# Block and sparse attention of a two-block transformer in steps of two heads: TensorE's order of scores, weight tile, transposes and sums

## What is computed

```
moba (8 heads), one block of 256 keys, so the selected part is empty:
  p = softmax(where(kpos <= qpos, q k^T * scale, -inf));  y_a = p v
nsa (8 heads), per head:
  o_cmp = softmax(q kc^T) vc                  15 compressed keys
  o_slc = softmax(q_rot k_slc^T) v_slc        all blocks are selected
  o_win = softmax(q_rot k_win^T) v_win        window of 512
  out   = g0 * o_cmp + g1 * o_slc + g2 * o_win
```

## Time and profile before

| | |
|---|---|
| median of 3 runs | 2458.36 us (2456.95 to 2459.53) |
| the profiled execution's own time | 2455.22 us |
| its span | 2453.6 us |
| TensorE busy | 2315.1 us (94%) |
| VectorE (DVE) busy | 1648.4 us (67%) |
| ScalarE (ACT) busy | 1225.6 us (50%) |
| TensorE's mean granted clock | 0.978 of full speed |
| DMA | 461.97 MB, mean 188 GB/s |

### The profile page before, as it was taken

The page is one execution under the profiler, slowest core; times in us unless marked ns, Lnnn a source line. Parts: engine busy times, 40 slices in busy tenths (PEclk is TensorE's granted clock), DMA queues, the critical chain, the costliest instruction groups (busy, mean ns, idle before and its releaser), DMA issues.

```text
span 2453.6 us, 40748 instructions
## 1 busy us (share of the span) xinstructions
PE 2315.1 (94%) x14828; PEld 2054.1 (84%) x14828; DVE 1648.4 (67%) x2387; ACT 1225.6 (50%) x1701; POOL 76.3 (3%) x143
## 2 busy tenths in 40 slices
PE   3999998899999999989899999999999999999999
PEld 2888987888887888879888889789888898898888
DVE  7888666567778787666576566656765666557665
ACT  3445466454445445565354455545544555465443
POOL 0100000000000000000000000000000000000000
PEclk9999998899999999999899999999999999999999
DMA  8876554445665874645445544333555353334553
GB/s 329 287 281 219 199 201 153 170 155 206 257 239 211 289 276 168 224 148 186 147 156 187 188 170 174 121 120 139 187 189 188 139 206 121 108 130 167 206 182 109
DMA packets 74827, 461.97 MB, mean 188 GB/s; under 512 B 8448, under 2 KB 8592, under 8 KB 28464
## 3 DMA queue, kind: packets, MB, share of 16 engines
q1 hardware_dynamic: 53712, 383.28, 43.2%
q0 software_dynamic: 19376, 72.00, 8.2%
q10 hardware_dynamic: 1584, 4.62, 0.5%
HBM read 458.82 MB, written 1.05 MB: 187 GB/s over the span
## 4 chain that ended last, share of the span: by engine, by line
PE 82%; DVE 5%; ACT 5%; issue 4%; DVEq 2%; DMA 1%; ACTq 1%
PE ps L713 20%; PE ps L439 15%; PE ps L441 15%; PE ps L440 15%; PE ps L715 10%; DVE wlo L1563 1%; DMA adat<-in_ada 1%; ACT whi L1056 1%; PE ps L547 1%; PE ps L529 1%; PE ps L561 1%; PE ps L594 1%; DVE bufA L1696 1%; DVEq L1665 1%; ACT set_a L1104 0%
## 5 line engine op out<-in xcount | busy, mean ns | idle before, releaser
L1563 DVE TENSOR_TENSOR wlo<-raw,whi 128x2048 fp32r<-128x2048 f32 x360 | 823.7, 2291 | 243.7 <-ACT whi L1056 226.7
L1056 ACT ACTIVATE whi<-raw 128x2048 fp32r<-128x2048 f32 x359 | 686.1, 1912 | 224.0 <-PE ps L441 220.1
L713 PE MATMUL ps<-hx,whi 128*128 128x512 f32 x2112 | 750.8, 399 | 10.5 <-DVE hx L1666 6.7
L715 PE MATMUL ps<-hx,wlo 128*128 128x256 f32 x2112 | 593.8, 281 | 0.0
L713 PEld LDWEIGHTS ps<-hx,whi 128*128 128x128 f32 x2112 | 398.3, 189 | 109.8 <-DVE hx L1666 7.2
L439 PE MATMUL ps<-hx,whi 128*128 128x256 f32 (+1 forms) x1424 | 423.0, 297 | 6.1 <-DMA blk<-in_block 2.9
L440 PE MATMUL ps<-hx,whi 128*128 128x256 f32 (+1 forms) x1424 | 408.6, 287 | 0.0
L441 PE MATMUL ps<-hx,wlo 128*128 128x256 f32 (+1 forms) x1424 | 408.1, 287 | 0.0
L715 PEld LDWEIGHTS ps<-hx,wlo 128*128 128x128 f32 x2112 | 400.3, 190 | 2.1
L439 PEld LDWEIGHTS ps<-hx,whi 128*128 128x128 f32 (+1 forms) x1424 | 278.9, 196 | 15.9 <-issue 8.0
L440 PEld LDWEIGHTS ps<-hx,whi 128*128 128x128 f32 (+1 forms) x1424 | 278.7, 196 | 4.7 <-issue 4.3
(11 more groups left out here) (274 smaller groups left out, 3043.5 us busy)
## 6 DMA issues: line engine op xcount, KB each, us to landing
raw<-in_w SPq DMA_DIRECT2D x360, 1024.0 KB, 4.8
adat<-in_ada POOLq DMA_DIRECT2D x128, 512.0 KB, 4.7
raw<-in_ada SPq DMA_DIRECT2D x4, 512.0 KB, 8.2
blk<-in_block POOLq DMA_DIRECT2D x2, 990.5 KB, 5.0
x<-in_x POOLq DMA_DIRECT2D x1, 1024.0 KB, 9.9
raw<-in_ada ACTq DMA_DIRECT2D x2, 512.0 KB, 14.8
set_b<-in_ada SPq DMA_DIRECT2D x2, 512.0 KB, 12.5
set_b<-in_ada ACTq DMA_DIRECT2D x2, 512.0 KB, 18.6
```

The costliest lines, as they stand in the source:

```text
L713: mm(ps[:, bank + i, :].rearrange("p (a s) -> p a s", a=2), whi[:, slot, col:col + P], hx[:, :, k, :], start=(k == 0), stop=False)
L715: last = mm(ps[:, bank + i, 0:S], wlo[:, slot, col:col + P], hhi[:, k, :], start=False, stop=(k == KD - 1))
L1056: A(whi[:, slot, :], raw[:, slot, :], ACT.Copy).then_inc(*T.counts("hi_ready"))
L1563: tt(wlo[:, slot, :], raw[:, slot, :], whi[:, slot, :].bitcast(F32), ALU.subtract)\
```

## The change

TensorE gets a second function, `attend_twos`, for block and sparse attention. An odd step has only what stands beside it. An even step s has the scores of s and s+1, what stands beside it, the turns of s-2 and s-1, and then the sums of s-4 and s-3. In sparse attention the tiles and rotations of TensorE's `beside_nsa` move from the odd steps to the even steps ahead of them. The programs of ACT, DVE, SyncE and GpSimd are the same; latent and differential attention still go through `attend`.

```diff
--- before.py
+++ after.py
@@ -597,6 +597,24 @@
                     mm(o[i][:, 128:256], ins.values(units[i], 1), bufC[:, i, 256:384], start=False, stop=True,
                        skip_group_check=True).then_inc(*T.counts("o_ready"))
 
+            def attend_twos(ins, beside, before=lambda u: None, first_turn=lambda: None):
+
+
+                for s in range(ins.units + 3):
+                    if s % 2:
+                        beside(s)
+                        continue
+                    if s < ins.units:
+                        scores(ins, (s, s + 1))
+                    if s == 2:
+                        first_turn()
+                    beside(s)
+                    if 2 <= s <= ins.units:
+                        turn(ins, s - 2)
+                        turn(ins, s - 1)
+                    if s >= 4:
+                        weigh(ins, s - 4, "pt_ready", before)
+
             def attend(ins, beside, before=lambda u: None, first_turn=lambda: None):
                 for s in range(ins.units + (2 if ins.fused else 3)):
                     if s < ins.units:
@@ -790,7 +808,7 @@
                         slot = tile()
                         features(open_fill(), slot, width=128, chunks=1).then_inc(*T.counts("tile_used"))
 
-                attend(moba, beside_moba)
+                attend_twos(moba, beside_moba)
                 pe.wait_ge(*T.nth("pj_out", T.n["fills"]))
 
                 def rotate_q(i):
@@ -974,14 +992,14 @@
                 pe.wait_ge(*T.nth("rope_done", T.n["rot_ready"]))
 
                 def beside_nsa(s):
-                    if s in (3, 5, 7, 9):
-                        i = (s - 3) // 2
+                    if s in (2, 4, 6, 8):
+                        i = (s - 2) // 2
                         rotate(c2("perm_half"), set_b[:, 2 * i:2 * i + 2, :], ps[:, 6, :])
-                    if s in (1, 3):
+                    if s in (0, 2):
                         project("tokens")
-                    elif s in (5, 7):
+                    elif s in (4, 6):
                         project("features")
-                    elif s in (9, 11, 13, 15):
+                    elif s in (8, 10, 12, 14):
                         merge_gate()
 
                 def compressed(u):
@@ -993,7 +1011,7 @@
                                         skip_group_check=True)
 
 
-                attend(nsa, beside_nsa, compressed, lambda: pe.wait_ge(*T.next("ct_out")))
+                attend_twos(nsa, beside_nsa, compressed, lambda: pe.wait_ge(*T.next("ct_out")))
                 pe.wait_ge(*T.nth("pj_out", T.n["fills"]))
                 wait_pairs()
                 pe.wait_ge(*T.nth("rope_done", T.n["rot_ready"]))
```

## The result

The kernel in steps of two heads takes 2511.32 us (median of 4 runs, 2511.07 to 2511.66) against 2458.82 us (4 runs, 2456.95 to 2459.53): ratio 1.0218, 95% interval 1.0203 to 1.0234, **52.5 us slower**. The forecast was 2504 us (2484 to 2520), that is +45.7 us. The profiled spans are 2509.7 and 2453.6 us, 56.1 us apart.

The account below looks back on a forecast made before the run. TensorE was taken as the bound, losing time where it stands still. Sparse waits 26.0, block waits 10.7 and clock 9 us gave +45.7 us on the profiled execution, 2500.9; with 3.1 us to the median, 2504 us, range 2484 to 2520.

Parts of the forecast that it names:

- Idle time inside sparse attention: Inside sparse attention: new TensorE waits ahead of rotations and scores in steps 4, 6, 8 and 12, 11.0 us per layer.
- the sum of 4.7 us: Sparse attention: time from the start of turn s-2 through turn, exponentials, norms and rope until the rope is done.
- The waits for norms that it saves: Sparse attention: the second turn would find its norms done behind a whole tile, saving 3.6 us per layer.
- The end of sparse attention: Last two turns, last sums and last pair would wait 3.0, 2.9, 1.0 and 0.95 us, together 7.85 against 2.28.
- Block attention: Middle costs nothing; last two turns and last sums wait 3.3, 3.7 and 1.3 us, 5.4 us more idle per layer.
- The clock: TensorE's clock halves behind new waits near or above 2 us: six falls taken, 9 us, bounded by 0 and 24.
- two in each sparse stretch: Clock falls assumed for each sparse attention stretch, beside one in each block stretch, six in all.
- the waits of step 6: Sparse attention: wait ahead of the rotation, put at 1.6 us and not among the waits that could lower the clock.
- all 16 waits: New waits near or above 2 us in block and sparse attention, eight per pair of stretches; all paying costs 24 us.
- Masks and ends pay, ropes don't: Rival: sparse rotations don't wait for ropes, only masks and the ends cost; 2485 us, chance 0.12.
- Every wait pays the clock: Rival: TensorE runs slow for 3 us after each of 16 new waits; 2519 us, chance 0.09.
- the forecast's own case: Waits in sparse attention and at block attention's ends plus six clock falls; 2504 us, bounds 2489 to 2519, chance 0.71.

Follow-up runs that it names:

- whole order: Against the kernel before: sparse attention alone in two-head steps, ordered even head's turn, rotation, sums, tile, odd head's turn; 2452.43 us, ratio 0.9975.
- the best one: The whole order plus matmuls on unused data in waits at the ends of block, latent and sparse attention and behind sparse; 2436.31 us, 0.9919 to the kernel before.
- rope first: The changed kernel with DVE's rope moved ahead of the odd head's norms in sparse attention; 2497.18 us, ratio 1.0160 to the kernel before.
- even turn first: The sparse-only kernel with the even head's turn alone moved ahead of rotation and tile; 2483.95 us, ratio 1.0110 to the kernel before.
- sparse-only kernel: The kernel before with the new two-head order in sparse attention alone, block attention in the old order; 2499.37 us, ratio 1.0164.

## Why the prediction was right

Size and sign were right, and the mechanism was the one forecast.

- *Idle time inside sparse attention.* Forecast 3.1, 1.6, 2.05, 2.2, 2.05; measured 3.02, 2.00, 2.09, 2.07, 2.09. Only the rotation of step 6 is off: it starts 5.06 us behind its turn, not 4.7. DVE's product with the gate starts 0.61 us behind the reciprocal there (1577.23 and 1577.84), in step 4 only 0.25 us, which is the difference. The handover from one engine to the next, which the prediction read as 0.1 us, is 0.04 us in the row that it cites; in the chain of step 4 it is 0.13 us (exponentials of 0.88 us start at 1564.84, DVE at 1565.85), so the sum of 4.7 us held. The experiments confirm both causes apart: moving the rope or the turn takes away the rotations' waits alone, moving the mask the scores' alone.
- *The waits for norms that it saves.* They went: no turn in the middle of the changed kernel waits. The gain showed only in the kernel with the whole order, 2.0 us per layer instead of 3.6, because its end is longer (1.21 + 1.27 + 0.97 us against 2.28) and 0.4 us of short waits are left inside.
- *The end of sparse attention.* Forecast 3.0, 2.9, 1.0, 0.95; measured 3.04, 2.24, 0.95, 0.97. The wait of the last turn is the one that is short, because of the clock: turn 15 starts 3.14 us behind turn 14 (forecast 3.3), but turn 14 ran 0.90 us at half clock, so more of that time counts as busy.
- *Block attention.* Forecast 3.3, 3.7, 1.3 with 5.4 us more idle per layer; measured 3.07, 3.50, 1.32 and 5.0. Its middle costs nothing, as said. In all, 35.2 us against 36.7.
- *The clock: this term was mis-sized.* Six falls of 1.5 us made 9 us; the busy time rose by 19.6 us, and filling the waits gave back 19.8. The block stretches came out as forecast, 1.33 + 1.93 = 3.3 us against 3. The step that was wrong is "two in each sparse stretch": 7.68 + 8.64 = 16.3 us against 6. The first sparse stretch has four separate slow places, and the last is long: the half clock lasts from the first of its four last waits into the next stage. That it lasts because only short pieces of work stand between these waits is likely, but not tested by itself. The prediction also left out the waits of step 6, which it put at 1.6 us; they came out at 2.00, and in one layer the clock fell there. Windows of the changed kernel, behind the waits at 1569.00, 1580.74 and 1617.67 and through its end:

```profile
1569.00:1572.00 3.00, 3.00 (x20) 2.52 (x21) 2.86 (x5) 0.73 (x1) 0.00 (x0) 1.00 0.00 0
1580.90:1583.90 3.00, 3.00 (x11) 2.25 (x11) 2.87 (x7) 1.03 (x1) 0.00 (x0) 0.56 0.02 5
1619.00:1622.00 3.00, 3.00 (x16) 3.00 (x16) 2.48 (x7) 2.61 (x4) 0.00 (x0) 0.50 0.03 5
1639.00:1652.50 13.50, 8.98 (x41) 5.28 (x42) 4.99 (x14) 5.14 (x12) 0.00 (x0) 0.51 0.21 79
```

  The second layer's windows, behind the same first two waits (3.02 and 2.01 us), have it the other way round:

```profile
2090.60:2093.60 3.00, 3.00 (x8) 1.97 (x9) 2.87 (x7) 0.70 (x1) 0.00 (x0) 0.50 0.00 0
2105.10:2108.10 3.00, 3.00 (x20) 2.52 (x21) 2.86 (x5) 1.18 (x1) 0.00 (x0) 1.00 0.03 5
```

  The Trainium skill, TensorE: Matmul & The Clock Gate, HAM oscillation, tells of a kernel that is throttled again in every wait between its short bursts of matmuls. That all 16 waits here would pay, 24 us, was the prediction's reading of it. The 19.8 us measured are nearer to it than to the forecast's 9, though in each layer one of the two waits above was followed by full clock, so not every wait pays.
- *The rivals.* "Masks and ends pay, ropes don't" fell with the rotations' waits. "Every wait pays the clock" overshot by 8 us; its 2519 is the full sum, 2458.4 + 60.7, and the rounding down that it names is not in it. The result lies halfway between it and the forecast's own case, and what speaks against it is the windows above, not the total. The forecast and the result lie 7 us apart: 10.6 too little for the clock, 1.5 too much idle time, and 2 us that the medians lie closer together than the four stretches. The last two went against the first, which is luck.

## What to carry to other kernels

Count from the instruction that frees a buffer, not from the one that computes: a reader moved behind a long tile holds back the writer, and all that stands behind the writer in the next engine's queue. Here a step of two heads was the better one only once each head's turn had other work ahead of it again. That the two turns stand side by side is not what cost inside the stretch: with the sums between them all five waits stayed, and with the even turn ahead of the tile those of the first two rotations went. Where a wait can't be avoided, matmuls on unused data can be put into it: here they gave back 20 us in the changed kernel and some 14 in the best one, with every dependence of the work left as it was.

## What the hardware showed that was not expected

- A wait's length did not decide alone whether the clock fell. In the changed kernel the one of 3.02 us left it at 1.00 in the first layer and had it at 0.50 behind it in the second; with that of 2.00 us it was the other way round. Removing the rotations' waits (rope first) hardly shortened the time at half clock (171.0 against 174.1 us), removing the scores' did (160.9). With the even turn first, which takes away the same two waits as rope first, it fell to 164.2 against 174.4 of the sparse-only kernel. Why, these runs don't tell. Each figure is of one execution, and the mean clock differs by up to 0.004 between the executions of one of these kernels, which is up to 20 us at half clock, so none of these differences is sure by itself.
- The same sequence of waits cost 93.55 and 97.52 us in two layers of one execution, by the clock alone. So in such a stretch some 4 us could not have been forecast from the lengths of the waits.
- With the waits filled, the changed kernel's sparse stretches were equal within 0.01 us (91.48 and 91.49); without, 1 us apart.
